# The end of the gated linear attention in another order: keys of one direction ahead, heads in pairs

## The reference

```python
    def step(S, inp):
        qc, kc, vc, ac = inp
        b = jnp.cumsum(ac, axis=2)
        diff = b[:, :, :, None, :] - b[:, :, None, :, :]
        decay = jnp.exp(jnp.where(mask, diff, -jnp.inf))
        attn = jnp.einsum('bhid,bhjd,bhijd->bhij', qc, kc, decay)
        o = attn @ vc + jnp.einsum('bhid,bhde->bhie', qc * jnp.exp(b), S)
        b_last = b[:, :, -1:, :]
        S_new = (jnp.exp(b_last[:, :, 0, :, None]) * S
                 + jnp.einsum('bhjd,bhje->bhde', kc * jnp.exp(b_last - b), vc))
        return S_new, o
...
    o = o_f + flip(o_b)
    o = o * lax.rsqrt(jnp.mean(o * o, axis=-1, keepdims=True) + EPS)
    o = o.transpose(0, 2, 1, 3).reshape(B_, L, GLA_VAL_WIDTH) * g_gla.astype(jnp.float32)
    o = (o * jax.nn.silu(r.astype(jnp.float32))).astype(h.dtype)
    y = jnp.concatenate([fourier_mix(u_f), o], axis=-1) @ w_out
```

## Time and profile before

| | us |
|---|---|
| median of 3 runs | 3046.67 (3045.13 to 3056.19) |
| the profiled execution, its own time | 3054.54 |
| its span | 3053.0 |
| last predicated copy of the scores ends | 1636.44 |
| first product of `pe_out2` on the chain | 1725.32 |

### The profile page before, as it was taken

How to read it: one execution, slowest core, us unless ns; L and a number is a source line. 1 busy time by engine, 2 the same in 40 slices (tenths; PEclk the granted TensorE clock), 3 DMA queues, 4 the chain that set the end, 5 groups by cost and what they waited for, 6 DMA issues and landing times.

```text
span 3053.0 us, 32412 instructions
## 1 busy us (share of the span) xinstructions
PE 2695.0 (88%) x13256; PEld 2231.6 (73%) x13256; DVE 1786.8 (59%) x2436; ACT 1081.7 (35%) x1419; POOL 32.5 (1%) x52
## 2 busy tenths in 40 slices
PE   5946599999849999899666999999999888899999
PEld 4845477888638888688365778888888766778887
DVE  6574668888778877721185255533552576465464
ACT  2242253233353235422222343312331555353242
POOL 0000000000010000000100000000000000000000
PEclk9966699999979999999855799999999999999999
DMA  8700037855215666221000012211221100123232
GB/s 307 243 22 2 1 109 252 286 180 187 69 43 179 201 203 202 91 93 55 14 1 1 24 53 63 68 64 56 63 67 58 51 27 15 55 83 106 88 102 85
DMA packets 80275, 295.06 MB, mean 97 GB/s; under 512 B 8944, under 2 KB 11632, under 8 KB 79872
## 3 DMA queue, kind: packets, MB, share of 16 engines
q1 hardware_dynamic: 80128, 292.99, 29.6%
HBM read 290.86 MB, written 2.10 MB: 96 GB/s over the span
## 4 chain that ended last, share of the span: by engine, by line
PE 79%; DVE 12%; ACT 5%; issue 2%; DMA 0%; POOL 0%; ACTq 0%; DVEq 0%
PE ps L311 65%; PE ps L337 3%; PE ps L733 2%; PE ps L1767 1%; PE ps L2236 1%; PE ps L2204 1%; DVE gatt L759 1%; DVE h_lo L519 1%; DVE w_lo L289 1%; DVE p_lo L2506 1%; DVE anm L2488 1%; DVE x L1343 0%; DVE x L1356 0%; PE ps L1942 0%; PE ps L1759 0%
## 5 line engine op out<-in xcount | busy, mean ns | idle before, releaser
L311 PE MATMUL ps<-h_hi,w_hi 128*128 128x512 f32 (+1 forms) x2416 | 815.8, 373 | 64.0 <-DVE w_lo L289 37.8
L311 PE MATMUL ps<-h_hi,w_lo 128*128 128x512 f32 (+1 forms) x2416 | 808.0, 370 | 0.0
L311 PE MATMUL ps<-h_lo,w_hi 128*128 128x512 f32 (+1 forms) x2416 | 804.1, 368 | 0.0
L289 DVE TENSOR_TENSOR w_lo<-w_raw,w_hi 128x1024 fp32r<-128x1024 f32 (+2 forms) x323 | 414.6, 1283 | 579.9 <-ACT w_hi L281 579.2
L281 ACT ACTIVATE w_hi<-w_raw 128x1024 fp32r<-128x1024 f32 (+2 forms) x323 | 357.4, 1107 | 885.3 <-PE ps L311 851.3
L311 PEld LDWEIGHTS ps<-h_hi,w_hi 128*128 128x128 f32 x2416 | 456.6, 189 | 152.8 <-DVE w_lo L289 42.1
L311 PEld LDWEIGHTS ps<-h_lo,w_hi 128*128 128x128 f32 x2416 | 457.4, 189 | 78.5 <-issue 2.2
L311 PEld LDWEIGHTS ps<-h_hi,w_lo 128*128 128x128 f32 x2416 | 456.2, 189 | 77.3
L311 PE MATMUL ps<-g_hi,w_hi 128*128 128x512 f32 (+1 forms) x880 | 297.5, 371 | 0.8 <-DVE w_lo L289 0.8
L311 PE MATMUL ps<-g_hi,w_lo 128*128 128x512 f32 (+1 forms) x880 | 297.0, 370 | 0.0
L311 PE MATMUL ps<-g_lo,w_hi 128*128 128x512 f32 (+1 forms) x880 | 294.9, 368 | 0.0
(11 more groups left out here) (372 smaller groups left out, 2854.3 us busy)
## 6 DMA issues: line engine op xcount, KB each, us to landing
w_raw<-in_up SPq DMA_DIRECT2D x176, 512.0 KB, 3.6
m_raw<-in_w_mod SPq DMA_DIRECT2D x96, 512.0 KB, 3.6
w_raw<-in_down SPq DMA_DIRECT2D x64, 704.0 KB, 4.2
m_raw<-in_ada_w SPq DMA_DIRECT2D x83, 512.0 KB, 4.7
w_raw<-in_in SPq DMA_DIRECT2D x39, 512.0 KB, 3.6
w_raw<-in_out SPq DMA_DIRECT2D x16, 512.0 KB, 3.5
m_start<-in_ada_w SPq DMA_DIRECT2D x13, 512.0 KB, 11.9
w_raw<-in_qkv SPq DMA_DIRECT2D x12, 512.0 KB, 3.5
```

What stands on the lines that cost most here:

```text
L289: dve.tensor_tensor(k.w_lo[s][:, 0:w], k.w_raw[s][:, 0:w], k.w_hi[s][:, 0:w].bitcast(F32), ALU.subtract).then_inc(*k.tick("w_lo", g))
L311: last = pe.matmul(ps[:, bank, 0:tn], a[:, c, :], b[:, c, t0:t0 + tn], start=c == 0 and n == 0, stop=c == kt - 1 and n == 2)
```

## The change

The tail is written in another order, in new functions, and some of its buffers are placed elsewhere.

- The decayed keys of the backward direction (1) now come first: their exponential, ACT L2033, stands right after the table load, waiting only for round 12 of the scores. They keep `gcomb`; those of direction 0 get the tile `spare`. The column of chunk ends is copied earlier, and its exponential has a tile of its own, `gexp`.
- Transposes go in groups of four to PSUM banks 6 and 7.
- PE's products for the states run four steps ahead of DVE: only step 4 waits for a state. The first state of a direction is a copy, and the zeroed states on POOL are gone, as are the products by a zero state (40 state products instead of 48).
- Heads are made in pairs, (0, 1) and (2, 3): the values' products of both (`pe_gl_values`), then the state products of both, alternating between them (`pe_gl_states`), in banks 0 to 2 for one and 3 to 5 for the other. Heads 0 and 1 have their values' products before the states exist.
- A head is copied out and squared in one instruction each instead of two; sum, root and the two parts of one head are staggered with those of the next. The split of the second weight tile of `pe_out2` moves ahead of the heads.

```diff
-    pool.wait_ge(*k.seen("q_decayed", "g"))
-    for d in range(2):
-        for f in range(2):
-            last = pool.memset(state[:, d, f * NC2 + GL_ORDER[d][0], :], 0.0)
-    last.then_inc(*k.tick("state_zero"))
...
+    if d == 0:
+        dve.tensor_copy(k.gends[:, 0, :].unsqueeze(2), e.rearrange("p (n c) -> p n c", c=CHUNK)[:, :, CHUNK - 1:CHUNK]
+                        ).then_inc(*k.tick("gl_ends"))
...
+    pe_gl_keys(k, 1)
+    pe_gl_values(k, 0, range(NC2))
+    pe_gl_add(k, 1)
+    pe_gl_keys(k, 0)
+    pe_gl_add(k, 0)
+    pe_gl_states(k, 0)
+    pe_gl_values(k, 2, range(2, NC2))
+    pe_gl_sum(k, 0)
+    pe_gl_values(k, 2, range(2))
+    pe_gl_states(k, 2)
+    for h in range(1, 4):
+        pe_gl_sum(k, h)
...
+def pe_gl_keys(k, d):
+    pe = k.nc.tensor
+    pe.wait_ge(*k.seen("kd", ("g", d)))
+    for b in range(3):
+        if d == 0 and b < 2:
+            pe.wait_ge(*k.seen("turned_out", ("gkd", 1, 2)))
+        elif b == 2:
+            pe.wait_ge(*k.seen("turned_out", ("gkd", d, 0)))
+        else:
+            pe.wait_ge(*k.seen("att", ("g", len(GL_STEPS) - 1, len(score_groups(GL_STEPS, len(GL_STEPS) - 1, 24)) - 1)))
+        for u, cols in enumerate(GL_FULL[4 * b:4 * b + 4]):
+            last = pe.matmul(k.ps[:, 6 + b % 2, u * P:(u + 1) * P], gl_decayed_keys(k, d)[:, cols], k.ident[:, :],
+                             is_transpose=True, start=True, stop=True)
+        last.then_inc(*k.tick("turn", ("gkd", d, b)))
...
+def gl_add_place(d, n):
+    return (6, 7, 2, 5)[2 * d + n // 2 % 2], n % 2
...
+def pe_gl_add(k, d):
+    pe = k.nc.tensor
+    pe.wait_ge(*k.seen("turned_out", ("gkd", d, 2)))
+    if d:
+        pe.wait_ge(*k.seen("att", ("g", len(GL_STEPS), len(score_groups(GL_STEPS, len(GL_STEPS), 24)) - 1)))
...
+        c, (bank, half) = GL_ORDER[d][n], gl_add_place(d, n)
+        if n == 4:
+            pe.wait_ge(*k.seen("state", ("g", d, 2)))
+        for h in range(4):
+            rows = slice((h % 2) * 64, (h % 2) * 64 + 64)
+            last = pe.matmul(k.ps[rows, bank, half * 256 + (h // 2) * P:half * 256 + (h // 2 + 1) * P], k.gkdt[d][:, (h // 2) * NC2 + c, rows],
+                             k.v2[:, c, h * P:(h + 1) * P], start=True, stop=True)
+        last.then_inc(*k.tick("state_add", ("g", d, n)))
...
+def gl_mixed_at(h, c):
+    return (h % 2) * 3 * BANK + (h // 2) * TALL + c * CHUNK
...
+def gl_mixed(k, h):
+    return k.ps[:, 0:6, :].rearrange("p b c -> p (b c)")[:, gl_mixed_at(h, 0):gl_mixed_at(h, NC2)]
...
+def pe_gl_values(k, h0, chunks):
+    pe = k.nc.tensor
+    if h0 == 0:
+        pe.wait_ge(*k.seen("att", ("g", len(GL_STEPS), len(score_groups(GL_STEPS, len(GL_STEPS), 24)) - 1)))
+    elif 0 in chunks:
+        pe.wait_ge(*k.seen("mixed_out", ("g", 1)))
+    for h in (h0, h0 + 1):
+        for c in chunks:
+            pe.matmul(gl_mixed(k, h)[:, c * P:(c + 1) * P], k.v2[:, c, h * P:(h + 1) * P], k.gatt[:, GL_PLACE[h, c], :],
+                      start=c == 0 or gl_mixed_at(h, c) % BANK == 0, stop=False)
...
+def pe_gl_states(k, h0):
+    pe, (e0, e1), state = k.nc.tensor, gl_views(k)[2], gl_views(k)[6]
+    if h0 == 0:
+        pe.wait_ge(*k.seen("q_decayed", "g"))
+        pe.wait_ge(*k.seen("state", ("g", 0, NC2 - 1)))
+    f = h0 // 2
+    adds = [(h, c, d) for c in range(NC2) for d in range(2) if GL_ORDER[d][0] != c for h in (h0, h0 + 1)]
+    ends = {gl_mixed_at(h, c) // BANK: (h, c, d) for h, c, d in adds}
+    for h, c, d in adds:
+        rows = slice((h % 2) * 64, (h % 2) * 64 + 64)
+        last = pe.matmul(gl_mixed(k, h)[:, c * P:(c + 1) * P], state[rows, d, f * NC2 + c, :],
+                         (e0, e1)[d][rows, f * TALL + c * CHUNK:f * TALL + (c + 1) * CHUNK], start=False, stop=(h, c, d) in ends.values())
+    last.then_inc(*k.tick("mixed", ("g", h0)))
...
+def pe_gl_sum(k, h):
+    pe = k.nc.tensor
+    pe.wait_ge(*k.seen("squared", ("g", h)))
+    if h:
+        pe.wait_ge(*k.seen("root_log", ("g", h - 1)))
+    for t0, tn, bank in segments(TALL):
+        last = pe.matmul(k.ps[:, 6 + bank, 0:tn], k.ones[:, :], gl_squares(k, h)[:, t0:t0 + tn], start=True, stop=True)
+    last.then_inc(*k.tick("summed", ("g", h)))
...
+def gl_head(k, h):
+    return gl_combs(k)[2 if h < 2 else 0][:, (h % 2) * TALL:(h % 2 + 1) * TALL]
...
+def gl_squares(k, h):
+    return k.gkdt[0][:, :, :].rearrange("p n c -> p (n c)")[:, (h % 2) * TALL:(h % 2 + 1) * TALL]
...
+    act.wait_ge(*k.seen("gl_ends"))
+    act.activation(k.gexp[:, :, :], k.gends[:, :, :], ACT.Exp, scale=s16).then_inc(*k.tick("end_decay", "g"))
+    act.wait_ge(*k.seen("scored", ("g", len(GL_STEPS) - 2, len(score_groups(GL_STEPS, len(GL_STEPS) - 2, 24)) - 1)))
+    act.activation(gl_decayed_keys(k, 1), e1, ACT.Exp, scale=s16).then_inc(*k.tick("kd_decay", ("g", 1)))
     act.wait_ge(*k.seen("kd_arg", "g"))
...
+    act.activation(gl_decayed_keys(k, 0), gl_decayed_keys(k, 0), ACT.Exp, scale=s16).then_inc(*k.tick("kd_decay", ("g", 0)))
+    act_gl_turned(k, 1)
     act.activation(e0, e0, ACT.Exp, scale=s16).then_inc(*k.tick("q_decay", ("g", 0)))
     act.wait_ge(*k.seen("q_arg"))
     act.activation(e1, e1, ACT.Exp, scale=s16).then_inc(*k.tick("q_decay", ("g", 1)))
-    act.activation(k.gends[:, :, :], k.gends[:, :, :], ACT.Exp, scale=s16).then_inc(*k.tick("end_decay", "g"))
+    act_gl_turned(k, 0)
+    act_split(k, BASE["out2"] + 1)
...
+        act.wait_ge(*k.seen("mixed", ("g", h // 2 * 2)))
+        act.activation(gl_head(k, h), gl_mixed(k, h), ACT.Copy).then_inc(*k.tick("mixed_out", ("g", h)))
         act.wait_ge(*k.seen("mixed_out", ("g", h)))
...
+        if h >= 2:
+            act.wait_ge(*k.seen("summed", ("g", h - 2)))
+        else:
+            act.wait_ge(*k.seen("state_add", ("g", 0, NC2 - 2)))
+        act.activation(gl_squares(k, h), gl_head(k, h), ACT.Square).then_inc(*k.tick("squared", ("g", h)))
         if h:
...
+            act_gl_root(k, h - 1)
+        if h >= 2:
+            act_high(k, "gla", 4 + h - 2, slice(0, TALL), gl_head(k, h - 2))
+    act_gl_root(k, 3)
+    for h in (2, 3):
+        act_high(k, "gla", 4 + h, slice(0, TALL), gl_head(k, h))
...
+def act_gl_turned(k, d):
+    act = k.nc.scalar
+    for b in range(3):
+        act.wait_ge(*k.seen("turn", ("gkd", d, b)))
+        got = k.ps[:, 6 + b % 2, :].rearrange("p (i t) -> p i t", t=P)
+        act.activation(k.gkdt[d][:, 4 * b:4 * b + 4, :], got, ACT.Copy).then_inc(*k.tick("turned_out", ("gkd", d, b)))
...
+def act_gl_root(k, h):
+    act = k.nc.scalar
+    act.wait_ge(*k.seen("summed", ("g", h)))
+    if h:
+        act.wait_ge(*k.seen("normed", ("g", h - 1)))
+    for t0, tn, bank in segments(TALL):
+        last = act.activation(k.rstd[:, t0:t0 + tn], k.ps[:, 6 + bank, 0:tn], ACT.Ln, scale=1.0 / P, bias=k.col("eps6"))
+    last.then_inc(*k.tick("root_log", ("g", h)))
+    act.wait_ge(*k.seen("root_log", ("g", h)))
+    act.activation(k.rstd[:, :], k.rstd[:, :], ACT.Exp, scale=-0.5).then_inc(*k.tick("root", ("g", h)))
...
+    kd0, kd1 = (gl_decayed_keys(k, d) for d in range(2))
+    dve.wait_ge(*k.seen("kd_decay", ("g", 1)))
+    dve.tensor_tensor(kd1, kd1, kk, ALU.mult).then_inc(*k.tick("kd", ("g", 1)))
+    dve.wait_ge(*k.seen("scored", ("g", steps, len(score_groups(GL_STEPS, steps, 24)) - 1)))
+    dve.tensor_tensor(v3(kd0), wide(k.gends[:, 0, :]), v3(e0), ALU.subtract).then_inc(*k.tick("kd_arg", "g"))
+    dve.tensor_tensor(v3(e1), wide(k.gends[:, 1, :]), v3(e1), ALU.subtract).then_inc(*k.tick("q_arg"))
+    dve.wait_ge(*k.seen("kd_decay", ("g", 0)))
+    dve.tensor_tensor(kd0, kd0, kk, ALU.mult).then_inc(*k.tick("kd", ("g", 0)))
     dve.wait_ge(*k.seen("q_decay", ("g", 0)))
     dve.tensor_tensor(e0, e0, q, ALU.mult)
...
+    dve.wait_ge(*k.seen("kd", ("g", 0)))
+    dve.wait_ge(*k.seen("end_decay", "g"))
+    dve_gl_states(k, 1)
     dve.wait_ge(*k.seen("q_decay", ("g", 1)))
     dve.tensor_tensor(e1, e1, q, ALU.mult).then_inc(*k.tick("q_decayed", "g"))
...
+    dve.wait_ge(*k.seen("q_decayed", "g"))
+    dve_gl_states(k, 0)
+    dve_split(k, BASE["out2"] + 1)
...
+        if h:
+            dve_low(k, "gla", 4 + h - 1, slice(0, TALL), gl_head(k, h - 1))
+    dve_low(k, "gla", 7, slice(0, TALL), gl_head(k, 3))
...
+def dve_gl_states(k, d):
+    dve, state = k.nc.vector, gl_views(k)[6]
+    for n in range(NC2 - 1):
+        c, nxt, (bank, half) = GL_ORDER[d][n], GL_ORDER[d][n + 1], gl_add_place(d, n)
+        dve.wait_ge(*k.seen("state_add", ("g", d, min(n | 1, NC2 - 2))))
+        if n:
+            dve.wait_ge(*k.seen("state", ("g", d, n)))
+        for f in range(2):
+            new, add = state[:, d, f * NC2 + nxt, :], k.ps[:, bank, half * 256 + f * P:half * 256 + (f + 1) * P]
+            if n:
+                at = f * NC2 + c
+                last = dve.scalar_tensor_tensor(new, state[:, d, at, :], k.gexp[:, d, at:at + 1], add, ALU.mult, ALU.add)
+            else:
+                last = dve.tensor_copy(new, add)
+        last.then_inc(*k.tick("state", ("g", d, n + 1)))
```

(24 more changed lines are left out.)

73 lines of the change are left out of this document (4 added, 69 removed).

## The result

The changed kernel took 2996.11 us (median of 4 runs, 2994.43 to 3006.4); the kernel before, run beside it, 3047.2 (median of 4). The ratio is 0.9836 with a 95% interval of 0.9812 to 0.986: 51.1 us less by the medians, where 42.4 less was forecast. The profiled execution took 2994.43 us, its span is 2993.1.

A forecast was written before the change was run, and what follows sets the result against it. PE bounds the kernel, but in the 88.88 us tail DVE, ACT and PE take turns. The new tail, 44.3 plus 2 us given as 46.5, saves 42.4: 3046.67 - 42.4 = 3004.3 us, range 2997 to 3019.

The forecast's parts named there:

- the clock: In the tail: PE's clock rises in two dense stretches of products, saving 42.4 us with it instead of 36.4.
- the allowance of 2 us for handovers: Added to the tail's 44.3 us for handovers not counted, giving 46.5.
- forecast, all low: Tail with PE's clock low throughout: 52.5 us, 36.4 less; as a rival 3010.3 us, chance 0.17.
- forecast, mixed: Tail with the clock high in two dense stretches: last sum free between 43.3 and 44.5 us, 44.3 taken.
- State products of two heads overlap: Heads of a pair: alternating state products overlap as scores do, 20 x 0.22 + 0.28 us at the low clock.
- rival (b): Heads: values' products keep 0.72 us, or state products don't overlap (7.0 or 8.4 us more); 3011 to 3019, chance 0.11.
- Values' products at half of 0.43: Values' products in a row cost 0.43 us each at the low clock, about half at the high, weights uncharged.
- They wait for nothing and fill a time in which PE idled.: First pair's 12 values' products, behind the backward transposes: 6.4 to 11.5 us at the low clock, in PE's idle time.
- The run-ahead of the additions: State additions: PE four steps ahead, waiting only before the fifth; backward four steps 11.5 to 14.9 us, DVE updates 0.63 each.
- Heads: Behind the second pair ACT is the bound: steps of 1.7, 1.9 and 2.5 us ahead of the last sum.
- Rival (c): Heads: the stagger gives nothing, they keep 52.4 us; only the states shrink, saving some 6 us, 3041, chance 0.06.
- Rival (d): Output product inherits a low clock, each tile taking 8.7 us more; all eight would end at 3074 us, chance 0.04.

The follow-up runs named there:

- the repeat: Changed kernel, no edit, profiled a second time: median 2996.27 us, ratio 0.9838, tail 40.33 us.
- The kernel with the old order and filler: Kernel before, order unchanged, with dense products that do no useful work added where PE waits in the tail: 3025.13 us, ratio 0.9927, tail 74.42.
- lockstep: Changed kernel with PE waiting for every state before its next products and DVE taking each addition singly: 3004.96 us, ratio 0.986, tail 49.40 us.
- the improved kernel: Changed kernel with first pair's values' products among forward additions, heads 2 and 3 copied before the roots, head 2's sum in other banks: 2991.47 us, again 2991.51.

## Why the prediction came out so

The direction and the mechanisms held; the size was 8.2 us short in the tail (46.5 forecast, 38.35 measured, and 44 to 50 named as the sign of being right). Two terms were mis-sized: the clock, some 6 us, and the allowance of 2 us for handovers. The low end of the range rests on a tail near 40 us; the measured one lies just beyond it. The milestones, in us from the last predicated copy:

| | forecast, all low | forecast, mixed | measured |
|---|---|---|---|
| backward additions done | 15.8 | 13.7 | 13.43 |
| last state | 25.0 | 22.9 | 20.60 |
| first pair's state products done | 29.7 | 27.6 | 23.23 |
| second pair done | 41.9 | 34.7 | 29.91 |
| last sum done | 52.5 | 44.3 | 38.35 |
| with the 2 us added | | 46.5 | 38.35 |

Two slips stand in the forecast's own sums, and neither decides anything. 44.3 and 2 make 46.3; 46.5 belongs to the 44.5 beside it. And in the case all at the low clock the steps on ACT behind the second pair (1.7, 1.9, 2.5 and a logarithm of 1.05) add up to 7.15 us, which puts the last sum's start near 49.1 and not 49.9, and its end near 51.7.

- **The clock.** I had it high in two stretches of dense products and low between them, for the forward transposes, the forward additions and the first pair's state products. In the first profile the windows show it at 1.00 from 1652 on without a return; in the repeat it fell once, to 0.78 in the last window before `pe_out2`. The high clock goes with 2.3 us at the last state and 2.1 more in the first pair (20 products in 2.50 us where I had 20 x 0.22 + 0.28); the sum behind the first pair costs 1.35 us and the last one 1.53, not 2.93, and the last one alone gives the 1.2 us behind the second pair. The kernel with the old order and filler shows that the clock was worth at least 14.5 us of the old tail; lockstep and no stagger show that it falls again when PE is made to pause. The clock is therefore no separate gain of the change: it is what the closed gaps bring along.
- **The 2 us for handovers.** They were not needed. The chain has short handovers between engines, 0.14 us ahead of the last sum, but where the clock was forecast rightly the milestones came out without an allowance (13.43 us where 13.7 stood), and ACT's steps behind the second pair took 6.91 us where their prices made 7.15. That the 0.28 us behind each last product covered them is my reading and no run shows it.
- **State products of two heads overlap.** Right: 0.125 us each at the high clock (0.23 in the block of 4.54 at the low one), and 0.22 at the high clock when they go head by head. That alternation pays is shown; whether by the halves or by the banks is not. This closes rival (b)'s second half.
- **Values' products at half of 0.43.** Right: 8 in 1.98 us, 4 in 0.89, 12 in 2.87, that is 0.22 to 0.25 each. This closes the first half of (b): no change of rows inside a block, no 0.29. The Trainium skill's rule (TensorE: Matmul & The Clock Gate, The mechanism), by which a weight load overlaps running products only if the row group differs, would add an estimated 0.21 us to each; all 24 together took 6.73 us, of which that rule alone would make 5.1, and the rows contradict it for these products. The same section of the Trainium skill also lets a load run ahead when it goes to the background weight buffer; that statement agrees with the 0.22 us.
- **"They wait for nothing and fill a time in which PE idled."** True and worth next to nothing: with them behind the additions the tail is 38.69 us where the changed kernel's three are 38.08, 38.35 and 40.33. The additions could have had that time, but giving it to them gained nothing either: the values' products must be done before the state products, and these start at 21.1 us with the products late and at 20.8 in the improved kernel, where they started at 20.7.
- **The run-ahead of the additions.** Right: 7.6 us up to the last state and 2.0 behind it, by the kernel in lockstep.
- **Heads.** The chain behind the second pair runs as I had it: head 2's copy and square, root 1's logarithm and exponential, head 0's high part, head 3's copy and square, root 2's logarithm, sum. It took 8.44 us, where I had 9.6 by 44.3 - 34.7. Rival (c), that the stagger gives nothing, is refuted by the 19.4 to 21.6 us of the kernel without it.
- **The output product.** Rival (d) did not come: L338 x96 takes 16.64 us (17.43 before), and from its start to the start of the next such block in the chain 83.4 us (84.1 before).

Not isolated by a run of its own: the states end 15.9 us earlier, of which the lockstep explains 7.6; that the directions go one after the other, with PE at backward keys while ACT and DVE make the forward ones, that POOL's step is gone, and the higher clock of the rest must bring the other 8.3 us. That is only a difference, and how it divides is open. And the pieces do not add up by design: each removal also costs clock.

## What to carry to other kernels

When several engines hand small pieces to each other, look first for the pattern "product, other engine, product" in the chain, and give PE a second independent piece (another head, the next steps' products) to stand between. Closing PE's gaps can pay twice: here many of the products between the pauses of lockstep and of no stagger ran at half the clock, and a sum cost 2.9 us in place of 1.5. So forecast the clock with the gaps of the new order, and let it stay high where they are gone. Group products that use the same part of the array, and where only half of it is used alternate halves, with a bank for each: here that took a block of 20 from 4.36 to 2.50 us. Where work only fills an idle time, its place in the list may matter little: here, with the same 12 products in three places, the first pair's state products started 20.4 to 21.8 us after the last predicated copy, and one kernel alone spanned 20.5 to 21.8.
